# Hybrid attention and DeltaNet layer, one core: attention steps of units 54 to 85 moved to units with a DeltaNet step, and side steps put in another order within a unit

## The reference

```python
def hybrid_mixer(h, w_in, ...):
    proj = h @ w_in
    qa, ka, va, qkv_dn, z_dn, b_dn, a_dn, gate_att, gate_dn = jnp.split(proj, split_at, axis=-1)
    y_att = moba_attention(...)                 # 8 heads of 64; with 512 tokens: causal softmax attention
    qkv_dn = jax.nn.silu(causal_depthwise_conv(qkv_dn, conv_w))
    o_dn = gated_delta_rule(...)                # chunked recurrence over a state of 64x64 per head
    o_dn = rms_norm(o_dn, dn_norm) * jax.nn.silu(z_dn)
    merged = (jax.nn.sigmoid(gate_att) * (y_att @ w_branch_att)
              + jax.nn.sigmoid(gate_dn) * (y_dn @ w_branch_dn))
    return merged @ w_out

x = x + rms_norm(hybrid_mixer(rms_norm(x), ...))
x = x + rms_norm(square(relu(rms_norm(x) @ w_mlp_in)) @ w_mlp_out)
```

## Time and profile before

| | |
|---|---|
| median of 3 runs | 753.53 us (753.53 to 753.84) |
| profiled execution | 753.69 us, its span 751.9 us |
| PE busy | 744.5 us (99%) |
| DVE, ACT, POOL busy | 418.1, 383.9, 322.6 us |
| mean granted TensorE clock | 0.998 |

### The profile page before, as it was taken

The page is one execution under the profiler, slowest core; times in us unless marked ns, Lnnn a source line. Parts: engine busy times, 40 slices in busy tenths (PEclk is TensorE's granted clock), DMA queues, the critical chain, the costliest instruction groups (busy, mean ns, idle before and its releaser), DMA issues.

```text
span 751.9 us, 12181 instructions
## 1 busy us (share of the span) xinstructions
PE 744.5 (99%) x4180; PEld 610.3 (81%) x4180; DVE 418.1 (56%) x627; ACT 383.9 (51%) x623; POOL 322.6 (43%) x294
## 2 busy tenths in 40 slices
PE   9999999999999999999999999999999999999996
PEld 7788778888877878788887988888888888888885
DVE  5796899980444545345702612211221777788795
ACT  6656842268554365635524833323332655555671
POOL 2357894435454754575446464445445000000002
PEclk9999999999999999999999999999999999999999
DMA  9336224577596688397941244556484775554652
GB/s 329 112 88 208 56 65 117 156 183 173 165 196 156 188 176 210 100 224 211 287 160 42 71 126 141 130 183 168 129 214 129 202 237 189 194 191 159 208 183 113
DMA packets 83214, 123.45 MB, mean 164 GB/s; under 512 B 5824, under 2 KB 44896, under 8 KB 83168
## 3 DMA queue, kind: packets, MB, share of 16 engines
q1 hardware_dynamic: 74384, 105.80, 43.9%
q0 software_dynamic: 8448, 16.78, 13.1%
q10 hardware_dynamic: 336, 0.28, 0.1%
HBM read 120.73 MB, written 35.67 MB: 208 GB/s over the span
## 4 chain that ended last, share of the span: by engine, by line
PE 93%; POOL 3%; ACT 2%; DVE 1%; issue 0%; ACTq 0%; POOLq 0%; DVEq 0%
PE bank L676 28%; PE bank L678 27%; PE bank L677 27%; POOL rsq L1955 2%; PE bank L901 1%; PE bank L924 1%; PE bank L911 1%; POOL w_lo L1961 1%; PE bank L865 1%; PE bank L829 1%; PE bank L697 1%; PE bank L706 1%; PE bank L876 1%; PE bank L933 1%; PE bank L973 0%; PE bank L703 0%
## 5 line engine op out<-in xcount | busy, mean ns | idle before, releaser
L1961 POOL TENSOR_TENSOR w_lo<-raw,w_hi 128x512 fp32r<-128x512 f32 x177 | 229.5, 1305 | 251.5 <-ACT w_hi L1113 249.7
L1113 ACT ACTIVATE w_hi<-raw 128x512 fp32r<-128x512 f32 (+2 forms) x214 | 144.9, 684 | 171.7 <-PE bank L678 160.1
L676 PE MATMUL bank<-h_hi,w_hi 128*128 128x512 f32 (+1 forms) x528 | 208.5, 395 | 0.1
L677 PE MATMUL bank<-h_lo,w_hi 128*128 128x512 f32 (+1 forms) x528 | 204.2, 387 | 0.0
L678 PE MATMUL bank<-h_hi,w_lo 128*128 128x512 f32 (+1 forms) x528 | 204.1, 386 | 0.0
L676 PEld LDWEIGHTS bank<-h_hi,w_hi 128*128 128x128 f32 x528 | 99.2, 188 | 25.0 <-issue 4.0
L678 PEld LDWEIGHTS bank<-h_hi,w_lo 128*128 128x128 f32 x528 | 99.2, 188 | 20.6
L677 PEld LDWEIGHTS bank<-h_lo,w_hi 128*128 128x128 f32 x528 | 99.3, 188 | 18.7
L1492 DVE SCALAR_TENSOR_TENSOR relu_sb<-bank,rs_row 128x512 f32<-128x512 f32 x32 | 20.6, 686 | 126.5 <-PE bank L678 114.8
L2092 POOL TENSOR_SCALAR ssh<-ssy 128x1 f32<-128x1 f32 x4 | 1.0, 238 | 151.6 <-ACT junk L1463 151.6
L676 PE MATMUL bank<-w_hi,h_hi 128*128 128x512 f32 x128 | 50.3, 393 | 0.1
(11 more groups left out here) (300 smaller groups left out, 1204.2 us busy)
## 6 DMA issues: line engine op xcount, KB each, us to landing
raw<-in_w_in SPq DMA_DIRECT2D x87, 256.0 KB, 3.2
raw<-in_w_mlp_in SPq DMA_DIRECT2D x62, 256.0 KB, 2.7
t_sum<-in_w_mlp_out POOLq DMA_DIRECT2D x12, 1024.0 KB, 10.7
raw<-in_w_mlp_out SPq DMA_DIRECT2D x26, 256.0 KB, 3.0
raw<-t_sum SPq DMA_DIRECT2D x26, 256.0 KB, 3.3
v_sum<-in_w_mlp_out SPq DMA_DIRECT2D x4, 1024.0 KB, 7.1
t_sum<-in_w_mlp_out SPq DMA_DIRECT2D x4, 1024.0 KB, 7.1
v_sum<-in_w_mlp_out POOLq DMA_DIRECT2D x4, 1024.0 KB, 11.5
```

Of the source, the lines that this page charges most:

```text
L676: pe.matmul(o, s_hi, m_hi, start=start, stop=False, skip_group_check=True)
L677: pe.matmul(o, s_hi, m_lo, start=False, stop=False, skip_group_check=True)
L1113: return a.activation(o, i_, ACT.Copy, scale=scale)
L1961: g.tensor_tensor(w_lo[:, slot, :], raw[:, slot, :], w_hi[:, slot, :].bitcast(F32), ALU.subtract).then_inc(lo_ready, 1)
```

## The change

Only the numbers in `AT` for `a1`, `an`, `a2`, `a3` and `ot`, and `rank`, are changed. No instruction's operands, no wait and no load is added or taken away; banks of side steps are renumbered as the order of their uses changes. `rank` may now name a single step: chunks 5 and 7 of `a2` come after `a3` of their unit.

```diff
-    "ot": (70, 76, 88, 90),
-    "a1": (49, 56, 59, 61, 64, 66, 69, 72, 75, 77, 81),
-    "an": (52, 57, 60, 62, 65, 68, 70, 74, 76, 79, 82),
-    "a2": (54, 59, 61, 63, 66, 69, 71, 75, 77, 79, 84),
-    "a3": (55, 61, 63, 65, 68, 70, 74, 76, 79, 81, 85),
+    "ot": (73, 79, 88, 90),
+    "a1": (49, 54, 56, 60, 62, 65, 68, 71, 74, 78, 81),
+    "an": (52, 55, 57, 61, 63, 66, 69, 72, 75, 79, 82),
+    "a2": (54, 56, 59, 62, 65, 68, 71, 74, 78, 81, 84),
+    "a3": (55, 57, 60, 64, 68, 70, 74, 76, 79, 83, 85),
...
-    rank = {..., "a3": 1, "a2": 12, ..., "sa": 6, ..., "oo": 5, "pa": 10, ...}
+    rank = {..., "a3": 8, "a2": 1, ..., "sa": 9, ("a2", 5): 10, ("a2", 7): 10, ..., "oo": 5, "pa": 5, ...}
-    return sorted(s, key=lambda x: (..., rank.get(x[1], 9)))
+    return sorted(s, key=lambda x: (..., rank.get((x[1], x[2]), rank.get(x[1], 9))))
```

More of the change, by code:

```diff
@@ L157, in side_steps @@
         s.append((TABLE[g][0] + (4 if GROUPS[g][1] == "f" else 8), "ev", g))
-    rank = {"ev": 0, "rw": 5, "an": 1, "bt": 16, "gm": 0, "vb": 20, "ma": 24, "mb": 9, "ot": 0, "a3": 1, "a2": 12, "ga": 10, "a1": 24, "sa": 6, "on": 24, "b1": 20, "pb": 4, "yp": 16, "zp": 0, "dec": 2, "gs": 24, "sb": 8, "gr": 24, "bi": 24, "ld": 24, "py": 5, "oo": 5, "pa": 10, "sc": 10, "b2": 1, "rt": 6, "bo": 3, "gk": 4, "kk": 12, "op": 12, "ap": 3, "ba": 10, "tv": 9, "cv": 8, "sg": 9}
-    return sorted(s, key=lambda x: (min(x[0], U_DN), x[0] if x[0] > U_DN else 0, rank.get(x[1], 9)))
+    rank = {"ev": 0, "rw": 5, "an": 1, "bt": 16, "gm": 0, "vb": 20, "ma": 24, "mb": 9, "ot": 0, "a3": 8, "a2": 1, "ga": 10, "a1": 24, "sa": 9, ("a2", 5): 10, ("a2", 7): 10, "on": 24, "b1": 20, "pb": 4, "yp": 16, "zp": 0, "dec": 2, "gs": 24, "sb": 8, "gr": 24, "bi": 24, "ld": 24, "py": 5, "oo": 5, "pa": 5, "sc": 10, "b2": 1, "rt": 6, "bo": 3, "gk": 4, "kk": 12, "op": 12, "ap": 3, "ba": 10, "tv": 9, "cv": 8, "sg": 9}
+    return sorted(s, key=lambda x: (min(x[0], U_DN), x[0] if x[0] > U_DN else 0, rank.get((x[1], x[2]), rank.get(x[1], 9))))
 def nth(u):
```

## The result

The changed kernel takes 770.11 us (769.6 to 771.18, 5 runs), the kernel before, on the same chip, 753.84 (753.53 to 754.1, 5 runs): a ratio of 1.0219, 95% interval 1.0208 to 1.0231. That is 16.3 us more, where 10.4 were forecast, and 2.6 us above the upper end of the range. The three forecast waits are there. The low clock that came with them cost 6.1 us, where 1.9 were forecast.

A forecast was written before the change was run, and what follows sets the result against it. The prediction took PE (TensorE) to bound the kernel: 753.5 us, plus waits of 3.9, 1.6 and 3.6, less 0.6 for fewer shape changes (+8.5), plus 1.9 for one clock fall, gave 763.9 us. Its range was 757.5 to 767.5.

The forecast's parts named there:

- What bounds the kernel: Whole program, units 54 to 90 too: PE sets the end, so any wait it gets moves the total by as much.
- The wait at unit 56: First matmul of unit 56: ACT does chunk 1's exponentials and scalings before evicting z_sb, so PE waits 3.9 us.
- The wait at unit 74: Scores a1[8] need a3[6]'s bank; DVE's copy stands behind oo[1], which waits for POOL: PE waits 3.6 us.
- The wait at unit 68: Scores a1[6] need a3[4]'s bank, copied by DVE after oo[0] and two evictions: PE waits 1.6 us.
- The clock: Behind the two long waits, units 56 and 74: one fall to half clock assumed, costing 1.9 us.
- The case of two falls: Three waits, clock falling in both long ones: 765.8 us, or 767.3 with each wait half a microsecond longer; chance 0.16.
- The changes of shape: PE's side steps, units 54 to 90: changes fall from 81 to 75, at 0.09 to 0.11 us each, saving 0.6 us.
- that only shape changes count: Units 54 to 90: the three waits together stay under 0.6 us, giving 752.9 us, at worst 753.5; chance 0.05.
- Only the wait at unit 56: The two waits on DVE vanish, leaving unit 56's: 756.8 us, or 758.7 with a fall of the clock; chance 0.12.
- That the clock never falls: All three waits at units 56, 68 and 74, with the clock staying full: 762.0 us; chance 0.27.

The follow-up runs named there:

- experiments three: The changed kernel with oo[1] behind a3[6] in unit 74, and a1[6] and its an a unit later (69, 70): 759.35 us.
- eight: The changed kernel with a1[6] and a1[8] a unit later (69, 75), their an at 70 and 76, DVE's order kept: 760.85 us.
- the part-filled kernel: The changed kernel with only 6, 4 and 6 useless extra products on PE at the start of its three waits: 767.15 us.
- the first experiment: The changed kernel with 17, 12 and 17 useless products on PE during its waits at units 56, 68 and 74: 763.99 us.
- the second experiment: The changed kernel with oo[1] behind a3[6] in unit 74 on DVE, PE's order unchanged: 764.12 us.

## Why the prediction was right in mechanism and wrong in size

- **What bounds the kernel** was right: PE, so that each wait reached the end in full.
- **The wait at unit 56**, 3.9 us forecast, was 3.94, with each step of ACT's chain that is read above within 0.1 us. It is there with one chunk moved in the old order (3.93) and goes when ACT has the evictions first: shown.
- **The wait at unit 74**, 3.6 forecast, was 3.98; the chain ran 0.3 longer than the sum. That the cause is DVE's copy behind an instruction that waits for POOL is shown: turning these two round removes it, with PE's order and the six uses of four banks as they are.
- **The wait at unit 68**, 1.6 forecast, was 2.77. The chain was right; the 0.7 for `oo`[0] on DVE was mis-sized. I took it from a row where POOL was idle; now POOL began its next split 0.03 us ahead, and it took 1.80. That PE's scores wait there for DVE's copy is in the trace, and the wait goes when they come a unit later (experiments three and eight); DVE's own order at this place was not changed in any run.
- **The clock** is the step that failed: "I take one: +1.9". The runs showed three falls and 6.1 us. First, I held a fall possible only for waits longer than the 2.95 us of the earlier trace rows; that row says after what idleness it once fell, not that less is safe, and 2.77 us brought one, 1.8 in the part-filled kernel too. Secondly, I took half of 3.8 us from the start as the price of each; the stretches at half clock were 3.4 or 6.8 us long, 1.7 to 3.2 us lost. The case of two falls, 0.16, was the nearest that I had, and none was as bad as what came. Of the 5.9 us by which the forecast rise fell short (16.3 against 10.4), 4.2 are the clock and 1.6 the waits: with the waits right and one fall, the forecast would still have been near 765.5. With the waits and falls as measured, the 753.8 measured beside them and the forecast 0.6 for the shapes, the same sum gives 753.8 + 10.7 + 6.1 - 0.6 = 770.0.
- **The changes of shape**, 0.6 us forecast, came out as 0.5 by the sum above and 0.3 with the waits filled (764.0 - 753.6 - 10.7). Both are what is left over in a sum, and smaller than the spread of the kernel before (753.26 to 754.06), so that the gain is not shown by a run. One reason for less than 0.6 is in PE's rows: the state product of 16 passes took 1.98 from start to start between `a3` and scores, where it took 1.70 between large matmuls (207.49 to 209.19 in the trace before). So what a change costs depends on what stands beside it. In PE's timeline of the changed kernel:

```profile
215.51 2.05 PE L865 MATMUL bank<-state,qk_dn 128*128 128x128 f32 x16
217.49 0.93 PE L901 MATMUL bank<-qk_att 64*128 64x128 f32 x8
```

- **The rivals:** that only shape changes count fell with the first row of PE's waits. Only the wait at unit 56 is the third experiment, 759.35, and not the change. That the clock never falls is the first experiment, 763.99, where 762.0 was worked out: the 2 us between are mostly the waits at units 68 and 74, 1.6 us longer than forecast.

## What to carry to other kernels

Where one table orders all engines, moving a step on the engine that bounds the kernel moves it on the others too: look at what then stands behind a wait on each in-order engine, above all evictions and bank copies of 0.3 us that the bounding engine needs. Packing side work to save 0.1 us per change of shape was worth nothing here against the 2.7 us of cover that each unit of large matmuls gives. And in these traces every wait of TensorE of 1.8 us or more in mid-program cost, besides its length, 1.7 to 3.2 us for the half clock that came with it, where the one of 1.28 us cost only its length (other runs than the profiled one had fewer or shorter low stretches with the waits filled in part); a forecast should hold both lengths of the low stretch possible for each such wait.

## What the runs showed of the hardware that I had not expected

- The granted clock fell to 0.50 behind a wait of 2.77 us, some 0.1 us after PE had begun to work again, and behind one of 3.94 us 0.6 us after, so that PE worked at half speed for 3.4 us without a pause; with others of 3.9 and 4.0 us it fell inside the wait, 0.8 to 2.1 us before its end (the kernel before with one chunk moved; unit 74 of the changed kernel; unit 56 in the second experiment), and stayed low for 6.7 or 6.8 us. It fell even with a wait of 1.8 us (the waits filled in part), not with one of 1.28.
- The same wait of 3.9 us at unit 56 cost 1.7 us of clock in the changed kernel, 2.4 in the second experiment, whose program is the same up to there, and 2.9 in the kernel before with one chunk moved. Of the five runs of the changed kernel, three had a mean granted clock of 0.990 (769.6 to 770.1 us) and two 0.988 (771.0 and 771.2).
- Matmuls of no use in the waits brought 6.1 us back.
- DVE's product of two SBUF operands took 1.80 us beside a POOL subtraction that began 0.03 us earlier, and 0.69 alone.
